# Dilated attention: values as weights in two column halves, output by features

## The chip, the cores and the metric

The kernel runs on one core of one Trainium2 chip, as one launch. The metric is the device time of one execution in microseconds (us); lower is better.

## The reference, cut to what matters

The kernel computes a fixed stack of layers for 256 tokens of width 1024: swiglu blocks, dilated attention, latent attention, windowed grid attention, a gated linear attention and two MLPs. The change lies in the dilated attention:

```
q, k, v = split(x @ w_in, 3)               # 3 groups x 16 heads x 64
q = rope(rmsnorm(q) * q_gain); k = rope(rmsnorm(k) * k_gain)
for g, (window, dilation) in ((128, 1), (512, 4), (2048, 16)):
    o_g, lse_g = softmax attention over t - j * dilation, j = 0 .. window / dilation
wts = softmax(stack(lse_g))                # over the three groups
y = (sum_g wts_g * o_g) @ w_out            # 256 x 1024
```

The weighted sum over the three groups equals one softmax over the scores of all three, with one maximum and one denominator per query and head. The kernel computes it so: 384 scores a row for the first 128 queries (three groups, one key block), 768 for the second 128 (two key blocks).

## The kernel before

Every engine has its own instruction stream, written out by hand in Python; the streams meet only at semaphores (`wait_ge` on a signal and key). Within an engine the order is strict. Nothing is planned at run time.

**Products.** Weights arrive from HBM in chunks of 1 MB. ScalarE rounds a chunk to a high part (`act_begin`, line 439), VectorE forms the low part (`dve_begin`, line 452), and TensorE runs three products for each tile (`mm3`). All products stand in the trace under line 466 (`mm`), all transposes under line 475 (`tr`). An fp32 product leaves two records in the trace, an fp32r product or a transpose one.

**Dilated attention** (lines 1153 to 1418). Four head groups hs of four heads. The loop runs hs from -1 to 3 and i from 0 to 9: at step i TensorE first runs the projection i of head group hs+1 (48 products of 256 columns; i // 3 is the dilation group, i % 3 is q, k or v), then the work of head group hs. So a period of ten steps holds nine projections for the next head group and the whole attention of this one; with hs = 3 there is none, and chunks of an unrelated modulation layer fill the steps 0, 2, 4, 6 (`FILL_DILATED`).

- q and k: ScalarE squares the projection (1285), VectorE sums over a head (1350), GpSimd makes the reciprocal root (1437 to 1446), VectorE scales out of PSUM (1372) and multiplies by the cosine (1374), GpSimd by the sine (1453, 1454), VectorE adds (1377). This is `rotate(hs+1, i)`; in VectorE's stream it is the last thing of step i. TensorE transposes the result (`turn`, at the steps of `DIL_TURN`, line 1139), ScalarE copies it to SBUF (1293).
- `dil_step` numbers eight attention steps s of a head group: pairs s0, s0+1 are two heads of one query block; s // 2 % 2 is the query block tb. At i = 0, 2, 4, 6 TensorE computes `scores` for the pair (the heads in the two row halves of the array), VectorE adds the mask and takes the maximum (1361, 1363), ScalarE exponentiates in place into `aSM` and leaves the row sums in `den` (1302).
- At i = 1, 3, 5, 7 TensorE transposes the exponentials (`turn_p`, three or six 128 x 128 tiles, in groups of three), for both steps of the pair. The groups and the q and k turns alternate between the PSUM banks 5 and 6 (`spare`). VectorE copies the first group to `aPT` (1385), ScalarE the second one (1311).
- `pv` (line 1224): the transposed probabilities are the weights (128 x 128), the values move (64 columns), three or six products per step; the output of all eight steps stands by tokens in bank 7. Step s0 is taken at the even step after, step s0+1 one step later, between the transposes of the next pair.
- At the end of each head group VectorE takes the reciprocal of the eight denominators (1411) and multiplies the output out of PSUM into `aO` (1415, two instructions).

**After the last head group** `attn_out_pe` (1113) turns `aO` to features: 16 transposes into banks 0 to 3, copied as high parts by ScalarE (1103) and low parts by VectorE (1110), then the output projection (96 fp32r products of four chunks in two halves; its first 48 need the tiles 0 to 3 alone).

`x_free`, `h_free` and `grid_sp` hold waits that keep later loads and writes off these buffers.

Of the kernel before, what the change touches and what calls it, by code (L numbers as in the profile page):

```python
# [149 lines left out]
class Program:  # L150
# [106 lines left out]
    def phase_views(self):  # L257
# [12 lines left out]
        self.aO = v(X0, 0, [128, 2048]).rearrange("p (b d) -> p b d", b=2)  # L270
        self.aT = [v(X1, 512 * i, [128, 512]) for i in range(4)]
# [681 lines left out]
    def x_free(self, tag):  # L953

        return {"dil": [(self.turned, ("residual", 0, 3)), (self.v_step, "tables")],
                "f1": [(self.turned, ("dilo", "o", 3))],
# [155 lines left out]

    def attn_out_pe(self, tag, O, ready, w_out):
        self.turn_o_pe(tag + "o", O, ready, 1)
        for half in range(2):
            self.pe_linear(w_out[:, half * 512:half * 512 + 512], self.x_of(tag + "o", 1), 4 * half, 256, (tag, "out", half))
            self.empties(range(4 * half, 4 * half + 4), (self.res, (tag, half)))

    def attn_out_act(self, tag, nxt, at):
        self.turn_o_act(tag + "o", 1)  # L1120
# [4 lines left out]
    def attn_out_dve(self, tag, nxt, at):  # L1125
        self.turn_o_dve(tag + "o", 1)
# [12 lines left out]
    DIL_TURN = {2: (0, 0), 4: (1, 0), 5: (0, 1), 7: (1, 1), 8: (0, 2), 9: (1, 2)}  # L1139
# [13 lines left out]
    def dilated_pe(self):  # L1153
# [57 lines left out]
        def turn_p(hs, s):  # L1211
            nonlocal spare
            u, n = s % 2, 3 * (s // 2 % 2 + 1)
            for c0 in range(0, n, 3):
                b = spare = 11 - spare
                pe.wait_ge(self.expd, ("dil", hs, s))
# [7 lines left out]
        def pv(hs, s):  # L1224
            hd, tb, _ = self.dil_step(s)
            u, hb = s % 2, hs % 2
            nk = tb + 1
            for i in range(3 * nk):
                o, kb = divmod(i, nk)
                g = self.dil_order(s)[o]  # L1230
# [3 lines left out]
                pe.wait_ge(self.evac, ("dil", "v", hs, g))  # L1234
                if s == 0:
                    self.pe_bank(7)
                m = self.mm(PS[:, 7, tb * 256 + hd * 64:tb * 256 + hd * 64 + 64], self.aPT[u][:, i * 128:i * 128 + 128],
                            self.aV[hb][:, g, kb * 256 + hd * 64:kb * 256 + hd * 64 + 64], i == 0, i == 3 * nk - 1)
            m.then_inc(*self.weighed.up(("dil", hs, s)))

        for hs in range(-1, 4):
            for i in range(10):
                if hs + 1 < 4 and i < 9:
                    proj(hs + 1, i)
                if hs + 1 < 4 and i in self.DIL_TURN:
# [3 lines left out]
                if hs >= 0 and i in (1, 3, 5, 7):  # L1249
                    turn_p(hs, i - 1)  # L1250
                    if i > 1:
                        pv(hs, i - 2)
# [3 lines left out]
                if hs >= 0 and i == 8:  # L1256
                    pv(hs, 7)
                if hs == 3 and i in FILL_DILATED:
                    self.pe_mods.send((0, 1))
            if hs >= 0:  # L1260
                self.empties([7], (self.o_done, ("dil", hs)))
        self.attn_out_pe("dil", self.aO, (self.o_done, ("dil", 3)), w_out)

    def dilated_act(self):
# [30 lines left out]
        def score(hs, s):  # L1295
# [4 lines left out]
            if hs:  # L1300
# [1744 lines left out]
```

## Time and profile before

| what | value |
|---|---|
| median of 3 runs | 2511.31 us (2510.83 to 2513.05) |
| profiled execution, its time | 2507.09 us |
| profiled execution, its span | 2505.8 us, mean granted TensorE clock 0.952 |
| TensorE products / weight loads busy | 94% / 86% |
| VectorE / ScalarE / GpSimd busy | 48% / 38% / 21% |
| HBM traffic | 341 MB read, 137 GB/s over the span |

A row of a timeline gives start, duration, engine, line, operation, output <- inputs with shapes, and how often; in brackets stands the time the engine idled before it, and what ended the wait. A matmul's duration contains its way through the array, so consecutive products overlap; what one costs is the distance between starts. PE is TensorE, DVE VectorE, ACT ScalarE, POOL GpSimd. "al" are tiles that share memory (`aSM`, `aPT`, `aV`, `aQK`, `aT`, `aO`), PS is PSUM. The granted clock is the share of 2.4 GHz.

### The profile page before, as it was taken

What the parts mean: (1) busy time and instruction counts of PE and PEld (TensorE: products, weight loads), DVE (VectorE), ACT (ScalarE), POOL (GpSimd) and SP (SyncE); (2) the same over time, 40 slices, a digit from 0 to 9 for tenths busy, and PEclk for the clock granted to TensorE, in tenths of its full rate; (3) what the DMA queues carried; (4) which work ended last, traced back from release to release, by engine and by line L of the source; (5) the groups of instructions that cost most, each with busy time, mean ns of one, the idle gap of its engine ahead of it and who ended that gap; (6) DMA issues with size and microseconds to landing.
All of it is one profiled execution on the core that took longest, in us unless ns stands there. A gap on an engine that the chain in (4) does not pass through costs nothing.

```text
span 2505.8 us, 38228 instructions
## 1 busy us (share of the span) xinstructions
PE 2349.1 (94%) x16869; PEld 2146.4 (86%) x16869; DVE 1211.3 (48%) x1560; ACT 958.5 (38%) x1128; POOL 517.3 (21%) x465
## 2 busy tenths in 40 slices
PE   6999999989999998889999899989999999888998
PEld 6998899979999997557999877877888887668998
DVE  5645566646555553445555355362123254544443
ACT  3433444434433442334444244333222224533442
POOL 2112434402211111220221111012211220220220
PEclk9999999989999998789999899979999989898998
DMA  6555433445555555676554310113233232113551
GB/s 241 177 171 174 136 129 124 135 169 185 182 171 185 185 169 182 217 250 227 180 185 156 105 34 18 35 68 102 100 101 101 86 95 92 59 51 93 182 181 67
DMA packets 205247, 344.75 MB, mean 138 GB/s; under 512 B 8845, under 2 KB 69498, under 8 KB 205082
## 3 DMA queue, kind: packets, MB, share of 16 engines
q1 hardware_dynamic: 205082, 342.31, 41.1%
q8 instruction: 133, 2.18, 0.4%
q14 instruction: 32, 0.26, 0.0%
HBM read 341.24 MB, written 1.05 MB: 137 GB/s over the span
## 4 chain that ended last, share of the span: by engine, by line
PE 81%; DVE 9%; POOL 4%; ACT 3%; issue 2%; SPq 0%; DMA 0%; DVEq 0%; POOLq 0%; ACTq 0%
PE PS L466 78%; PE PS L475 3%; DVE WL L452 3%; ACT WH L439 1%; POOL small L1444 1%; DVE XL L623 1%; POOL TMP L1453 1%; DVE XL L992 0%; DVE al L988 0%; POOL small L1442 0%; DVE TMP L1372 0%; POOL TMP L1454 0%; DVE TMP L1377 0%; DVE al L1901 0%; DVE al L1361 0%
## 5 line engine op out<-in xcount | busy, mean ns | idle before, releaser
L452 DVE TENSOR_TENSOR WL<-raw,WH 128x2048 fp32r<-128x2048 f32 (+2 forms) x281 | 651.4, 2330 | 711.1 <-ACT WH L439 711.0
L466 PE MATMUL PS<-XH,WH 128*128 128x256 f32 (+1 forms) x2336 | 700.7, 300 | 22.9 <-DVE WL L452 14.3
L466 PE MATMUL PS<-XL,WH 128*128 128x256 f32 (+1 forms) x2336 | 694.9, 297 | 0.0
L466 PE MATMUL PS<-XH,WL 128*128 128x256 f32 (+1 forms) x2336 | 694.6, 297 | 0.0
L439 ACT ACTIVATE WH<-raw 128x2048 fp32r<-128x2048 f32 (+2 forms) x281 | 518.9, 1858 | 360.5 <-PE PS L466 359.9
L466 PEld LDWEIGHTS PS<-XH,WH 128*128 128x128 f32 x2336 | 454.1, 194 | 36.6 <-DVE WL L452 15.1
L466 PEld LDWEIGHTS PS<-XL,WH 128*128 128x128 f32 x2336 | 454.5, 195 | 10.0
L466 PEld LDWEIGHTS PS<-XH,WL 128*128 128x128 f32 x2336 | 453.8, 194 | 10.2
L466 PE MATMUL PS<-WH,XH 128*128 128x256 f32 (+2 forms) x944 | 288.3, 305 | 17.8 <-DVE XL L623 8.5
L466 PE MATMUL PS<-WL,XH 128*128 128x256 f32 (+2 forms) x944 | 279.5, 296 | 0.0
L466 PE MATMUL PS<-WH,XL 128*128 128x256 f32 (+2 forms) x944 | 279.2, 296 | 0.0
L466 PE MATMUL PS<-HH,WH 128*128 128x256 f32 x960 | 272.0, 283 | 1.6 <-DVE WL L452 1.6
L466 PE MATMUL PS<-HH,WL 128*128 128x256 f32 x960 | 271.7, 283 | 0.0
L466 PE MATMUL PS<-HL,WH 128*128 128x256 f32 x960 | 271.7, 283 | 0.0
L466 PE MATMUL PS<-al,al 128*128 128x64 f32 (+8 forms) x1376 | 225.4, 342 | 14.8 <-DVE al L2903 4.8
L466 PEld LDWEIGHTS PS<-al,al 128*128 128x128 f32 (+4 forms) x1376 | 164.8, 197 | 63.0 <-issue 37.0
L466 PEld LDWEIGHTS PS<-WH,XH 128*128 128x128 f32 x944 | 186.6, 198 | 36.3 <-issue 22.3
L466 PEld LDWEIGHTS PS<-WL,XH 128*128 128x128 f32 x944 | 187.0, 198 | 2.5
L466 PEld LDWEIGHTS PS<-WH,XL 128*128 128x128 f32 x944 | 186.7, 198 | 2.5
L466 PEld LDWEIGHTS PS<-HH,WH 128*128 128x128 f32 x960 | 184.3, 192 | 1.8 <-DVE WL L452 1.8
L466 PEld LDWEIGHTS PS<-HL,WH 128*128 128x128 f32 x960 | 184.3, 192 | 0.0
L466 PEld LDWEIGHTS PS<-HH,WL 128*128 128x128 f32 x960 | 184.3, 192 | 0.0
(225 smaller groups left out, 2608.7 us busy)
## 6 DMA issues: line engine op xcount, KB each, us to landing
raw<-in_ffn_w_in SPq DMA_DIRECT2D x88, 1024.0 KB, 5.0
raw<-in_w_mod SPq DMA_DIRECT2D x48, 1024.0 KB, 5.1
raw<-in_ffn_w_out SPq DMA_DIRECT2D x40, 1024.0 KB, 4.9
raw<-in_a_w_in SPq DMA_DIRECT2D x36, 1024.0 KB, 4.9
raw<-in_w_mlp_in SPq DMA_DIRECT2D x32, 1024.0 KB, 5.4
raw<-in_w_mlp_out SPq DMA_DIRECT2D x32, 1024.0 KB, 5.0
raw<-in_gla_w_in SPq DMA_DIRECT2D x12, 1024.0 KB, 5.1
raw<-in_attn_w_qkv SPq DMA_DIRECT2D x6, 1024.0 KB, 5.2
```

The source lines that it names most:

```text
L439: act.e.activation(self.WH[q % NW][:, 0:nk * nn], self.raw[j % NRAW][:, 0:nk * nn], ACT.Copy).then_inc(*self.hi.up(j))
L452: dve.e.tensor_tensor(self.WL[j % NRAW][:, 0:nk * nn], self.raw[j % NRAW][:, 0:nk * nn], wh.bitcast(F32), ALU.subtract).then_inc(*self.lo. ...
L466: return self.pe.e.matmul(out, l, r, start=start, stop=stop, skip_group_check=skip)
L475: return self.pe.e.transpose(out, i, self.ident if n == 128 else self.CST[0:n, IDENT:IDENT + n])
L623: dve.e.scalar_tensor_tensor(self.XL[slot][:, k, :], R[:, k, :], self.COL[:, at + k:at + k + 1], self.XH[slot][:, k, :].bitcast(F32), ALU. ...
L1444: pool.e.tensor_tensor(rs, rs, self.MH[:, 0:8], ALU.pow).then_inc(*self.p_step.up(key("pow")))
L1453: pool.e.tensor_tensor(q[:, :, :, 0:32], x[:, :, :, 32:64], bc(0, 32), ALU.mult)
```

## The change

- `pv` takes a pair of steps at once, one step of i later than the first of them could be. The values are now the weights (128 x 64), the probabilities move (128 columns). The even head writes the partitions 0 to 63 of bank 7 and the odd one 64 to 127, so the two lie in the column halves of the array, their products taken in turn. The output stands by features: the same number of products as before.
- As the denominators are per token, the probabilities are divided before they are transposed: `scale` on VectorE takes a reciprocal of two columns and multiplies `aSM` of both steps in place; it stands ahead of everything else at i = 1, 3, 5, 7. `turn_p` on TensorE waits for it instead of the exponential. The reciprocal and the two products at the end of each head group leave VectorE.
- The q turn of the first dilation group moves from i = 2 to i = 3, and `turn_p` of the first step of a pair now stands before the q or k turn of that i.
- ScalarE copies the output of head groups 0 to 2 into `aOT`; high and low parts of these six tiles are made at i = 1, 3, 5 of the last head group, those of the last two straight from bank 7. The 16 transposes before the output projection are gone, for the latent attention they stay.

The core of the diff:

```diff
@@ -1110,20 +1111,35 @@
+    def split_o_act(self, tag, g, h, O, ready):
+        for signal, key in ready:
+            self.act.wait_ge(signal, key)
+        self.act.e.activation(self.XH[h][:, 2 * g:2 * g + 2, :], O, ACT.Copy).then_inc(*self.xh.up((tag, 2 * g)))
+    def split_o_dve(self, tag, g, h, O):
+        self.dve.wait_ge(self.xh, (tag, 2 * g))
+        self.dve.e.tensor_tensor(self.XL[h][:, 2 * g:2 * g + 2, :], O, self.XH[h][:, 2 * g:2 * g + 2, :].bitcast(F32), ALU.subtract).then_inc(*self.xl.up((tag, 2 * g)))
+        self.xl.name((tag, 2 * g + 1))
     def attn_out_pe(self, tag, O, ready, w_out):
-        self.turn_o_pe(tag + "o", O, ready, 1)
+        if O is not None:
+            self.turn_o_pe(tag + "o", O, ready, 1)
         for half in range(2):
...
     def attn_out_act(self, tag, nxt, at):
-        self.turn_o_act(tag + "o", 1)
+        if tag == "lat":
+            self.turn_o_act(tag + "o", 1)
         for half in range(2):
...
     def attn_out_dve(self, tag, nxt, at):
-        self.turn_o_dve(tag + "o", 1)
+        if tag == "lat":
+            self.turn_o_dve(tag + "o", 1)
         for half in range(2):
@@ -1136,7 +1152,7 @@
-    DIL_TURN = {2: (0, 0), 4: (1, 0), 5: (0, 1), 7: (1, 1), 8: (0, 2), 9: (1, 2)}
+    DIL_TURN = {3: (0, 0), 4: (1, 0), 5: (0, 1), 7: (1, 1), 8: (0, 2), 9: (1, 2)}
...
@@ -1213,7 +1229,7 @@
                 b = spare = 11 - spare
-                pe.wait_ge(self.expd, ("dil", hs, s))
+                pe.wait_ge(self.v_step, ("dil", "scaled", hs, s))
                 self.pe_bank(b)
...
                     m = self.tr(PS[:, b, i * 128:i * 128 + 128], self.aSM[u][:, (c0 + i) * 128:(c0 + i) * 128 + 128])
@@ -1221,45 +1237,47 @@
-        def pv(hs, s):
-            hd, tb, _ = self.dil_step(s)
-            u, hb = s % 2, hs % 2
+        def pv(hs, s0):
+            hb, tb = hs % 2, s0 // 2 % 2
             nk = tb + 1
-            for i in range(3 * nk):
-                o, kb = divmod(i, nk)
-                g = self.dil_order(s)[o]
+            if s0 == 0:
+                self.pe_bank(7)
+            for s in (s0, s0 + 1):
                 pe.wait_ge(self.emptied, ("dil", "p", hs, s))
...
                     pe.wait_ge(self.evac, ("dil", "p", hs, s))
-                pe.wait_ge(self.evac, ("dil", "v", hs, g))
-                if s == 0:
-                    self.pe_bank(7)
-                m = self.mm(PS[:, 7, tb * 256 + hd * 64:tb * 256 + hd * 64 + 64], self.aPT[u][:, i * 128:i * 128 + 128],
-                            self.aV[hb][:, g, kb * 256 + hd * 64:kb * 256 + hd * 64 + 64], i == 0, i == 3 * nk - 1)
-            m.then_inc(*self.weighed.up(("dil", hs, s)))
+            for i in range(3 * nk):
+                o, kb = divmod(i, nk)
+                for s in (s0, s0 + 1):
+                    hd, _, _ = self.dil_step(s)
+                    pair, j = divmod(hd, 2)
+                    g = self.dil_order(s)[o]
+                    pe.wait_ge(self.evac, ("dil", "v", hs, g))
+                    m = self.mm(PS[64 * j:64 * j + 64, 7, pair * 256 + tb * 128:pair * 256 + tb * 128 + 128], self.aV[hb][:, g, kb * 256 + hd * 64:kb * 256 + hd * 64 + 64],
+                                self.aPT[s % 2][:, i * 128:i * 128 + 128], i == 0, i == 3 * nk - 1, True)
+                    if i == 3 * nk - 1:
+                        m.then_inc(*self.weighed.up(("dil", hs, s)))
...
                     proj(hs + 1, i)
+                if hs >= 0 and i in (1, 3, 5, 7):
+                    turn_p(hs, i - 1)
                 if hs + 1 < 4 and i in self.DIL_TURN:
...
                 if hs >= 0 and i in (1, 3, 5, 7):
-                    turn_p(hs, i - 1)
-                    if i > 1:
-                        pv(hs, i - 2)
                     turn_p(hs, i)
...
                     pv(hs, i - 2)
-                if hs >= 0 and i == 8:
-                    pv(hs, 7)
                 if hs == 3 and i in FILL_DILATED:
...
             if hs >= 0:
-                self.empties([7], (self.o_done, ("dil", hs)))
-        self.attn_out_pe("dil", self.aO, (self.o_done, ("dil", 3)), w_out)
+                self.empties([7], (self.xl, ("dilo", 6)) if hs == 3 else (self.evac, ("dil", "o", hs)))
+        self.attn_out_pe("dil", None, None, w_out)
@@ -1297,8 +1315,6 @@
             act.wait_ge(self.v_step, ("dil", "neg", hs, s))
-            if hs:
-                act.wait_ge(self.v_step, ("dil", "recip", hs - 1))
             act.e.activation(SM, SM, ACT.Exp, bias=nm[:, u:u + 1], accum_out=den[:, tb * 4 + hd:tb * 4 + hd + 1]).then_inc(*self.expd.up(("dil", hs, s)))
...
         def turn_p(hs, s):
@@ -1309,6 +1325,9 @@
             act.e.activation(self.aPT[s % 2][:, 384:768], PS[:, b, 0:384], ACT.Copy).then_inc(*self.evac.up(("dil", "p", hs, s)))
+        def split(g):
+            self.split_o_act("dilo", g, 1, self.aOT[:, 2 * g:2 * g + 2, :], [(self.evac, ("dil", "o", g)), (self.lin, ("dil", 3, 8))])
...
             for i in range(10):
@@ -1328,6 +1347,15 @@
                     self.fill_act(0)
+                if hs == 3 and i in (1, 3, 5):
+                    split(i // 2)
+            if hs >= 0:
+                o = PS[:, 7, :].rearrange("p (k t) -> p k t", k=2)
+                if hs == 3:
+                    self.split_o_act("dilo", 3, 1, o, [(self.weighed, ("dil", 3, 7)), (self.lin, ("dil", 3, 8))])
+                else:
+                    act.wait_ge(self.weighed, ("dil", hs, 7))
+                    act.e.activation(self.aOT[:, 2 * hs:2 * hs + 2, :], o, ACT.Copy).then_inc(*self.evac.up(("dil", "o", hs)))
         self.attn_out_act("dil", "f1", 16)
@@ -1384,11 +1412,22 @@
+        def scale(hs, s0):
+            hd, tb, _ = self.dil_step(s0)
+            dve.wait_ge(self.expd, ("dil", hs, s0 + 1))
+            dve.e.reciprocal(rd[:, 0:2], den[:, tb * 4 + hd:tb * 4 + hd + 2]).then_inc(*self.v_step.up(("dil", "recip", hs, s0)))
+            dve.wait_ge(self.v_step, ("dil", "recip", hs, s0))
+            for s in (s0, s0 + 1):
+                SM = self.aSM[s % 2][:, 0:384 * (tb + 1)]
+                dve.e.tensor_scalar(SM, SM, rd[:, s - s0:s - s0 + 1], None, ALU.mult).then_inc(*self.v_step.up(("dil", "scaled", hs, s)))
         self.past_norm = None
...
                 if paired:
+                    scale(hs, i - 1)
                     turn_p(hs, i - 1)
...
                     self.dve_begin()
@@ -1405,16 +1444,9 @@
                     self.dve_mods.send(1)
-            if hs < 0:
-                continue
-            dve.wait_ge(self.weighed, ("dil", hs, 7))
-            dve.e.reciprocal(rd, den).then_inc(*self.v_step.up(("dil", "recip", hs)))
-            dst = self.aO[:, :, hs * 256:hs * 256 + 256].rearrange("p b (h d) -> p b h d", h=4)
-            dve.wait_ge(self.v_step, ("dil", "recip", hs))
-            for tb in range(2):
-                t = dve.e.tensor_tensor(dst[:, tb], PS[:, 7, tb * 256:tb * 256 + 256].rearrange("p (h d) -> p h d", h=4),
-                                        rd[:, 4 * tb:4 * tb + 4].unsqueeze(2).to_broadcast([128, 4, 64]), ALU.mult)
-            t.then_inc(*self.o_done.up(("dil", hs)))
+                if hs == 3 and i in (1, 3, 5):
+                    self.split_o_dve("dilo", i // 2, 1, self.aOT[:, i - 1:i + 1, :])
+        self.split_o_dve("dilo", 3, 1, PS[:, 7, :].rearrange("p (k t) -> p k t", k=2))
         self.attn_out_dve("dil", "f1", 16)
```

## Rows read from the trace of the kernel before

**Rows 1.** The page, part 1: busy time, share of the span, instructions.

```profile
PE 2349.1 (94%) x16869; PEld 2146.4 (86%) x16869; DVE 1211.3 (48%) x1560; ACT 958.5 (38%) x1128; POOL 517.3 (21%) x465
```

**Rows 2.** Busy time by stretch: length, busy (instructions), PEclk, DMA share, GB/s.

```profile
373.00:447.00 74.00, 72.14 (x618) 69.97 (x616) 48.07 (x68) 34.13 (x48) 29.93 (x36) 1.00 0.39 129
...
545.90:552.50 6.60, 6.53 (x30) 6.36 (x30) 0.57 (x2) 0.98 (x2) 0.00 (x0) 0.50 0.00 0
...
557.00:563.00 6.00, 6.00 (x52) 6.00 (x52) 3.68 (x3) 2.43 (x3) 0.00 (x0) 1.00 0.00 0
```

**Rows 3.** Waits of TensorE, 366 to 440 us: total, times, longest.

```profile
PE PS L475 <- ACT al L1311: 1.5, 1, 1.5
```

**Rows 4.** Timeline of TensorE, one period.

```profile
372.55 0.94 PE L466 MATMUL PS<-al,al 64*128 64x128 f32 x12
373.42 0.39 PE L466 MATMUL PS<-WH,XH 128*128 128x256 f32 x1
...
379.26 0.82 PE L475 MATMUL PS<-CST,al 128*128 128x128 f32 x6
...
437.59 2.79 PE L466 MATMUL PS<-al,al 128*128 128x64 f32 x24
440.22 0.61 PE L475 MATMUL PS<-CST,TMP 128*128 128x128 f32 x4
```

**Rows 5.** Timeline of VectorE, the same period.

```profile
379.39 0.69 DVE L1377 TENSOR_TENSOR TMP<-TMP,al 128x512 f32<-128x512 f32 x1 [1.39 <-POOL TMP L1454]
...
414.18 0.69 DVE L1377 TENSOR_TENSOR TMP<-TMP,al 128x512 f32<-128x512 f32 x1 [1.37 <-POOL TMP L1454]
...
427.28 0.69 DVE L1377 TENSOR_TENSOR TMP<-TMP,al 128x512 f32<-128x512 f32 x1 [1.40 <-POOL TMP L1454]
...
430.21 0.69 DVE L1350 TENSOR_REDUCE small<-al 128x8 f32<-128x512 f32 x1 [0.23 <-ACT al L1285]
...
436.93 0.69 DVE L1377 TENSOR_TENSOR TMP<-TMP,al 128x512 f32<-128x512 f32 x1 [1.39 <-POOL TMP L1454]
```

**Rows 6.** Timeline of VectorE and TensorE, last head group, step i = 7.

```profile
545.23 0.55 DVE L1385 COPY al<-PS 128x384 f32<-128x384 f32 x1
545.92 1.51 PE L475 MATMUL PS<-CST,al 128*128 128x128 f32 x6 [5.11 <-DVE al L1385]
```

**Rows 7.** The chain that ended last: start, us, what; one period, then the end.

```profile
398.03 5.75 PE PS L466 x48
...
430.28 0.62 PE PS L466 x6
...
437.76 2.63 PE PS L466 x24
...
547.44 5.03 PE PS L466 x24
552.49 0.21 DVE small L1411
...
552.73 0.77 DVE al L1415 x2
...
553.54 3.59 PE PS L475 x16
557.12 42.96 PE PS L466 x359
```

**Rows 8.** Timeline of TensorE: a fill by modulation.

```profile
521.55 1.06 PE L466 MATMUL PS<-raw,CS 128*32 128x512 f32 x8
```

**Rows 9.** Instructions by line and shape, whole span: busy, mean ns.

```profile
L1686 DVE TENSOR_SCALAR al<-al,small 128x384 f32<-128x384 f32 x2 | 0.8, 416 | 16.2 <-POOL small L1796 16.2
...
L1686 DVE TENSOR_SCALAR al<-al,small 128x256 f32<-128x256 f32 x2 | 0.7, 346 | 0.0
```

**Rows 10.** Timeline of ScalarE, the period of group 4.

```profile
394.58 0.18 ACT L1302 ACTIVATION_READ_ACCUMULATOR al<-al,small 128x1 f32 x1
...
440.86 0.60 ACT L1293 ACTIVATE al<-PS 128x512 f32<-128x512 f32 x1 [1.74 <-PE PS L475]
```

More of the change, by code:

```diff
@@ L270, in phase_views @@
         self.aO = v(X0, 0, [128, 2048]).rearrange("p (b d) -> p b d", b=2)
+        self.aOT = self.tiles(v(X0, 0, [128, 2048]))
         self.aT = [v(X1, 512 * i, [128, 512]) for i in range(4)]
@@ L955, in x_free @@
         return {"dil": [(self.turned, ("residual", 0, 3)), (self.v_step, "tables")],
-                "f1": [(self.turned, ("dilo", "o", 3))],
+                "f1": [(self.xl, ("dilo", 5))],
                 "f2": [(self.lin, ("f1", "up", 5))],
@@ L2240, in grid_sp @@
     def grid_sp(self):
-        self.sp.wait_ge(self.o_done, ("dil", 3))
+        self.sp.wait_ge(self.xl, ("dilo", 6))
         self.sp.e.dma_start(self.CST[:, 0:1024], self.A["const"][:, MASK_C:MASK_C + 1024]).then_inc(*self.ld_masks.up("grid"))
```

## The prediction

> **What bounds the kernel now.** I read the page, then the busy time by stretch, the waits of TensorE, and the timelines of one 74 us period of the dilated attention. TensorE's matmuls are busy 94% of the span [rows 1]. A period (attention of head group hs beside the nine projections of hs+1) repeats every 74 us with TensorE busy 72.14 of them, at the full clock (granted 1.00, 2.4 GHz) [rows 2]; there are three. In a period TensorE waits 1.5 us at one place [rows 3], and nowhere else as long as half of that. So in these periods the instructions in TensorE's queue set the time, and whatever delays one of them longer than those waits adds to it. VectorE is busy 48 us, but its order is fixed, and it waits for GpSimd inside every rotation: it finishes rotate(0) at 380.08 where TensorE finished the projection of i=1 at 379.26 [rows 4, 5]. Today that costs nothing, since the transposes of the probabilities need only the exponential. The last head group has no projections beside it: there TensorE waits 5.11 us for VectorE's copy of step 6, its clock is 0.50 (1.2 GHz) behind that, and after the last value product stand 4.6 us before the output projection [rows 2, 6, 7].
>
> **The value products.** 72 records a period (two per product; 3 products per step with one key block, 6 with two). The eight steps cost 4 x 0.62 + 4 x 1.3 = 7.7 us: six records take 0.62, twelve half of the 24 in 2.63 [rows 7], which the timeline shows as 2.79 with the end of the last one [rows 4]. After: 128 moving columns instead of 64, weights of 64 columns, two heads side by side in the array's halves. Such a form is not in the trace. Nearest rows: the scores, which pair two heads in the row halves with the same 128 moving columns: 12 records from 372.55 to the next product at 373.42, 0.87 us [rows 4]; and modulation's four column quarters, eight records of 512 columns in 1.06 us, near a quarter of the 3.4 they would need one by one, two passes each at 2.4 GHz, 0.43 a record [rows 8]. I take 0.9 us for a pair of one-block steps and, for twice the records with one entry and exit of some 0.3 us, 1.5 us for a pair of two-block steps: 2 x 0.9 + 2 x 1.5 = 4.8 us, a gain of 2.9 us a period. Bounds: nothing overlaps, 72 records of 0.107 us or 7.7 (gain 0); perfect overlap, half of it, 3.85 (gain 3.85).
>
> The Trainium skill speaks against it a little: "TensorEngine Tiling (Array Packing)", section Tiling Modes, says that a change of the tiling mode drains the array. Every pair would pay that on entry and exit. The scores' 0.87 us already holds two changes of mode, so the sum stays; had it to be paid on top, the gain would be nearer to the lower bound.
>
> **The scaling on VectorE.** Added per pair: a reciprocal (0.21, the wait behind it makes 0.24 [rows 7]) and two in-place multiplications of 384 or 768 elements. The nearest row is the multiplication of line 1686, SBUF to SBUF by a column: 0.416 us for 384 elements, 0.346 for 256 [rows 9]; 128 elements more cost 0.07, so 768 cost 0.416 + 3 x 0.07 = 0.63. Starts follow each other some 0.08 earlier. So step s0 is ready 0.7 us (0.95 with two blocks) after the scaling begins, VectorE is free after 0.95 (1.35). Bounds: free (0) and the PSUM copy's pace, 0.55 for 384 [rows 6] and near 0.95 for 768. Removed: one reciprocal and two multiplications out of PSUM at the end of each head group, 1.0 us of VectorE [rows 7]; added on ScalarE one 0.6 us copy of the outputs per head group, behind a product long done and beside the next projection: nothing, with several us idle there as cover.
>
> **Where TensorE now waits, for one period** (before, after, by shifting the rows):
> - i=1. The scaling stands behind rotate(0): starts 380.00, step 0 ready 380.72; TensorE asked at 379.26. Wait 1.5. All behind it moves 1.3 to 1.5, rotate(1) too.
> - i=2. The q turn (0.45) leaves, the pair costs 0.9 instead of 0.62: -0.15. Projection 3 now ends 395.4.
> - i=3. The exponential of step 3, 394.76 before [rows 10], comes at 396.06, since VectorE reaches the masks 1.3 later. Scaled step 2: 397.0, wait 1.6. Six transposes until 397.7. The q turn now stands here: its bank needs VectorE's copy (from 397.6, since three transposes end 0.5 us after their start, six taking 0.82 with starts 0.11 apart [rows 4], to 398.1), it runs to 398.57. ScalarE, in order, copies the turn (its copy starts 0.64 behind the turn, 440.22 to 440.86, and takes 0.5 before the next can start [rows 4, 10]), squares projection 3 (0.5) and only then empties (0.5) the bank that step 3 needs: 400.3. Step 3 is done at 400.95; before, the projection behind it stands in the chain from 398.03 [rows 7], and its first product began 0.25 earlier, beside the end of the transposes: 397.78: +3.2 in all, +2.0 by this step.
> - i=4 and 5. Rotate(3) ends near 407.1 (its square comes late, 399.9, then 7.3 as the shortest such rotation shows, 430.21 to 437.62 [rows 5]). It pushes rotate(4) from 414.87 to 416.05; scaled step 4 is ready 416.7, TensorE asks at 415.4. Wait 1.3, and 0.35 more for the one bank, in place of step 3's product (1.3): +0.4.
> - i=6: +0.15. i=7: rotate(6) ends 431.5, scaled step 6 almost in time (0.15), but turn, square and evacuation queue on ScalarE as at i=3 (1.7), less step 5's product: +1.05.
> - i=8: one pair of 1.5 for the 24 records in 2.63: -1.1.
>
> Sum 1.5 - 0.15 + 2.0 + 0.4 + 0.15 + 1.05 - 1.1 = +3.85 us a period, three periods +11.5. The 2.9 us of TensorE work saved are already in it.
>
> **The last head group and its end.** Up to step 6 the scaling's waits (about 1 us a pair) are paid by the shorter products and the fills of modulation as cover: 0. At i=7 VectorE is free at 545.23 as before; steps 6 and 7 are scaled at 546.1 and 546.6; transposes, two copies and evacuations at the half clock bring step 7's probabilities to 549.6. The product pair, 24 records, takes 3.0 us where it took 5.03 at that clock: until 552.7, as before 552.47. Then the output projection starts at once, where it stood until 557.12 behind 0.24 + 0.8 + 3.59 us [rows 7]: the transposes of the outputs are gone, and the split of the last two tiles lies beside the first 5.76 us of the projection, as long as one of 48 products [rows 7]. But the clock stays low until about 557 (it did after the wait of 5.11; the new wait is 6.9), so 4.4 us earlier are worth half: 2.1. The first six tiles' splits move into i=1, 3, 5 (0.6 on ScalarE, 0.7 on VectorE): they lie beside the fills. The mask load on SyncE waits for a later signal, far ahead of its use: nothing.
>
> Sum: +11.5 - 2.1 = +9.4 us. The profiled execution took 2507.1 us (span 2505.8), 4.2 below the median 2511.3; on that the forecast is 2520.7.
>
> **Rivals.**
> - *TensorE's work decides (faster).* Place: i=1, 3, 5, 7 of each period. If the scaling is hidden, the four groups keep 4 x 2.9 and the end gives 2 to 4.6: -14 to -16 us, about 2496. It decides where the waits added per period stay under the 2.9 saved. For it: VectorE idles 26 us a period [rows 2]. Against: it idles inside rotations, ahead of the scaling, not behind; the 1.5 us at i=1 needs no estimate beyond 0.7. 0.14.
> - *Even.* The bank queue at i=3 and 7 costs only half (ScalarE takes the evacuation first, or the shift of rotate(3) is absorbed): 3 x 1.5 - 2.1 = +2.4 us: 2513.7. 0.16.
> - *The clock falls in each period.* In 395.4 to 400.3 TensorE would stand 3.8 us. Rows show 0.50 for 6.6 us behind the wait of 5.11 us and 1.00 again from 557 on, while the period with the 1.5 us wait stays at 1.00 [rows 2, 3, 6]. If it falls once a period for as long as those 6.6 us, half of that is lost: 3 x 3.3 = +10 more, 2531. The Trainium skill, "TensorE: Matmul & The Clock Gate", section What's actually happening, calls the low clock the default that activity lifts; by that rule alone the low level would come back with these pauses; the rows show it behind the long one only. 0.12.
> - *The change's new form brings no overlap in the column halves.* Products cost 7.7 again: i=6 and 8 lose 1.35 more a period, the end 2: +6, 2527. It lies inside the forecast's sign. 0.08.
>
> **How the numbers follow.** Forecast as such 0.50; rivals as given. The forecast's own range is 2514 to 2528 (1 to 1.8 us a period either way from the scaling's and pair's bounds). With the others, 2504 to 2532 leaves out the faster rival's core and little above. Slower by over 0.2% (5 us, about what a measurement can tell): 0.50 of the forecast less 0.04 for its lower edge, the clock's 0.12, the missing overlap's 0.08 and a quarter of the even case, 0.04: 0.70. Within: the rest of these two, 0.16. Faster: 0.14.
>
> **What would show it.** Right: periods near 78 us; per period new waits of TensorE before transposes for VectorE's multiplication (1.5 at i=1) and for ScalarE's evacuation (1.7 at i=3 and 7); product pairs at 0.9 and 1.5; multiplications 0.42 and 0.63; no transposes between last product and projection, with the clock low across it. Wrong: periods under 74 us, or waits at i=3 without ScalarE in them.

## The result, and the profile after

The kernel with the change takes 2533.34 us (median of 4: 2527.25, 2529.35, 2537.32, 2537.54), the kernel before beside it 2511.07 (2510.68 to 2513.05): ratio 1.0079 with a 95% interval of [1.0055, 1.0103] (the two medians by themselves give 1.0089), 22 us slower. The forecast said slower, 2520.7 us; the median lies 1.3 us above its range. Run again later, five times beside nine runs of before, the same kernel took 2523.15 (2518.75 to 2525.74) against 2508.64: 1.0052 [1.0039, 1.0065], 14.5 us slower. Two of the four first runs, the profiled one among them (2537.54 and 2537.32), thus held some 12 us more than the slowest of those five.

The profiled run took 2537.54 us, 30.4 more than before's 2507.09. By stretches, from the same instruction to the same instruction in both traces:

| stretch | before | after | difference |
|---|---|---|---|
| up to the first exponential of the dilated attention | 300.7 | 303.2 | +2.5 |
| period 1, exponential to exponential | 73.97 | 79.96 | +6.0 |
| period 2 | 73.95 | 79.22 | +5.3 |
| period 3 | 68.67 | 75.11 | +6.4 |
| from there to the last weight load of the stage | 45.6 | 41.6 | -4.0 |
| grid attention, load to load, which the change doesn't touch | 141.4 | 155.3 | +13.9 |
| all the rest | | | +0.3 |

(Period 3 is short in both, as the first exponential of the last head group has no projection ahead of it.) So the dilated attention itself costs +13.7 us: +17.7 in three periods, -4.0 in the last head group. The +2.5 ahead of it lies before the attention of the first head group and need not be the change's: the traces of all kernels here start that exponential between 300.7 and 303.3 us, the kernel before reordered (e12) at 303.1.

Page of after, part 1 (answers to [rows 1]):

```profile
PE 2359.9 (93%) x16853; PEld 2144.0 (85%) x16853; DVE 1226.2 (48%) x1596; ACT 960.0 (38%) x1131; POOL 514.3 (20%) x465
```

The page hardly shows it: the shares are those of before. It takes the stretches. Busy time by stretch of after (columns as in [rows 2]): the three periods, then stretches of low clock in them (the four falls, the one of period 3 at i = 3 first), the end of the last head group, then one stretch of the grid attention:

```profile
303.24:383.20 79.96, 72.58 (x614) 68.04 (x613) 51.70 (x78) 34.52 (x48) 28.78 (x37) 0.96 0.36 119
383.20:462.42 79.22, 71.84 (x614) 67.47 (x613) 51.76 (x78) 34.59 (x48) 28.79 (x37) 0.98 0.36 120
462.42:537.53 75.11, 66.94 (x564) 61.91 (x566) 44.43 (x74) 28.57 (x44) 27.75 (x34) 0.95 0.37 123
...
487.50:490.90 3.40, 2.63 (x13) 2.66 (x14) 2.40 (x3) 1.71 (x4) 2.11 (x4) 0.51 0.03 9
409.00:412.40 3.40, 3.35 (x16) 3.38 (x17) 2.68 (x3) 1.81 (x2) 2.83 (x4) 0.51 0.00 0
327.10:333.90 6.80, 5.15 (x26) 4.78 (x24) 4.26 (x5) 3.77 (x5) 3.29 (x5) 0.50 0.22 72
525.10:528.50 3.40, 3.40 (x18) 3.40 (x17) 1.68 (x3) 0.49 (x1) 2.43 (x4) 0.50 0.04 14
...
562.60:572.80 10.20, 5.53 (x36) 4.72 (x36) 5.45 (x8) 1.78 (x4) 0.00 (x0) 0.50 0.26 90
...
1569.60:1600.30 30.70, 30.35 (x122) 21.86 (x120) 13.45 (x61) 10.01 (x30) 0.00 (x0) 0.50 0.00 1
```

Two things differ from before. TensorE is idle 7.4 us of a period instead of 1.9. And the granted clock of a period is no longer 1.00: it is 0.50 for 6.8, 3.4 and 6.8 us of the three. In the grid attention one stretch of 30.7 us runs at 0.50 with TensorE busy throughout; before is at 1.00 in that stage.

Where TensorE idles in period 2, its waits (answers to [rows 3]):

```profile
PE PS L476 <- ACT al L1327: 3.3, 2, 1.7
PE PS L476 <- DVE al L1423: 2.9, 3, 1.4
PE PS L476 <- DVE al L1413: 1.1, 3, 0.4
```

7.3 us, of the three kinds that the forecast named: the multiplication (line 1423), VectorE's copy that empties the one free bank (1413), ScalarE's evacuation behind turn and square (1327). One by one, timeline of TensorE in period 3:

```profile
468.42 0.88 PE L476 MATMUL PS<-CST,al 128*128 128x128 f32 x6 [1.25 <-DVE al L1423]
...
484.70 0.88 PE L476 MATMUL PS<-CST,al 128*128 128x128 f32 x6 [1.42 <-DVE al L1423]
485.99 0.63 PE L476 MATMUL PS<-CST,TMP 128*128 128x128 f32 x4 [0.41 <-DVE al L1413]
488.27 1.51 PE L476 MATMUL PS<-CST,al 128*128 128x128 f32 x6 [1.65 <-ACT al L1327]
...
505.07 0.55 PE L476 MATMUL PS<-CST,al 128*128 128x128 f32 x3 [0.27 <-DVE al L1423]
...
506.37 0.52 PE L476 MATMUL PS<-CST,al 128*128 128x128 f32 x3 [0.31 <-DVE al L1413]
...
522.17 0.63 PE L476 MATMUL PS<-CST,TMP 128*128 128x128 f32 x4 [0.41 <-DVE al L1413]
524.45 0.92 PE L476 MATMUL PS<-CST,al 128*128 128x128 f32 x6 [1.65 <-ACT al L1327]
...
532.91 1.53 PE L467 MATMUL PS<-al,al 128*64 128x128 f32 x24
```

i = 1, 3, 5, 7 in turn. And ScalarE at i = 3, why the bank is late: turn copy, square, evacuation, one after the other.

```profile
486.66 0.60 ACT L1311 ACTIVATE al<-PS 128x512 f32<-128x512 f32 x1 [1.06 <-PE PS L476]
487.15 0.59 ACT L1303 ACTIVATE al<-PS 128x512 f32<-128x512 f32 x1
487.63 0.50 ACT L1327 ACTIVATE al<-PS 128x384 f32<-128x384 f32 x1
```

What was added and made cheaper, by line and shape, period 2:

```profile
L467 PE MATMUL PS<-al,al 128*64 128x128 f32 x72 | 4.8, 278 | 0.0
...
L1423 DVE TENSOR_SCALAR al<-al,small 128x768 f32<-128x768 f32 x4 | 2.3, 618 | 0.1
...
L1423 DVE TENSOR_SCALAR al<-al,small 128x384 f32<-128x384 f32 x4 | 1.5, 418 | 0.1
```

The end of the last head group, timeline of TensorE (answers to [rows 6, 7]):

```profile
566.50 3.15 PE L476 MATMUL PS<-CST,al 128*128 128x128 f32 x12 [6.71 <-DVE al L1423]
570.32 2.76 PE L467 MATMUL PS<-al,al 128*64 128x128 f32 x24 [0.67 <-ACT al L1327]
573.01 0.39 PE L467 MATMUL PS<-XH,WH 128*128 128x256 f32 x1
```

The projection starts right behind the last value products, as meant, and the clock is back at 1.00 when it starts. (In the later profile of the same kernel, e14, it comes back 1.9 us into the projection.)

### The profile page after: what moved, and what is told of

Read it like the earlier page. It is cut to its first block, busy times and chain, and to the rows that moved or that the text cites. A ratio compares the mean times of both kernels' runs of the same rounds, so it can differ in the third digit from the quotient of the medians.

```text
span 2536.2 us, 38232 instructions
## 1 busy us (share of the span) xinstructions
PE 2359.9 (93%) x16853; PEld 2144.0 (85%) x16853; DVE 1226.2 (48%) x1596; ACT 960.0 (38%) x1131; POOL 514.3 (20%) x465
## 3 DMA queue, kind: packets, MB, share of 16 engines
HBM read 341.24 MB, written 1.05 MB: 135 GB/s over the span
## 4 chain that ended last, share of the span: by engine, by line
PE 80%; DVE 9%; POOL 5%; ACT 4%; issue 2%; SPq 0%; DMA 0%; DVEq 0%; POOLq 0%; ACTq 0%
PE PS L467 76%; PE PS L476 4%; DVE WL L453 3%; POOL small L1476 1%; ACT WH L440 1%; POOL TMP L1485 1%; DVE XL L624 1%; DVE TMP L1400 0%; POOL TMP L1486 0%; DVE TMP L1405 0%; DVE XL L993 0%; DVE small L1378 0%; POOL small L1474 0%; DVE al L1389 0%; DVE al L989 0%
## 5 line engine op out<-in xcount | busy, mean ns | idle before, releaser
L467 PE MATMUL PS<-al,al 128*128 128x64 f32 (+9 forms) x1376 | 220.1, 358 | 13.7 <-DVE al L2930 7.4
L467 PEld LDWEIGHTS PS<-al,al 128*128 128x128 f32 (+4 forms) x1376 | 154.4, 195 | 67.0 <-issue 41.4
```

Source lines behind the costliest of these rows:

```text
L467: return self.pe.e.matmul(out, l, r, start=start, stop=stop, skip_group_check=skip)
```

## The experiments

**Theories.** A: the fixed order of the queues. The multiplication stands behind a whole rotation, and the turn ahead of the second group of transposes; these make the waits, and moving the two makes them go. B: the work itself costs (VectorE's added time, or a product form without overlap), wherever it stands. C: the clock falls because of the new stands, or by itself.

To compare the runs I split the middle one of the three periods (first exponential of a head group to that of the next) into TensorE's waits, half of the time at clock 0.50 (what that level costs a busy TensorE), and the rest, which is TensorE's own work. The split is good to about 1 us, since some of the low time falls into waits. Within that, the rest is the same wherever the work is the same (68.6 to 70.3 with the paired products in turn, 72.0 to 72.6 with the products of before), so nothing else sets the period. The last two columns are for the whole stage: the time at 0.50 in all three periods, and the time from the first exponential to the output projection. Times of whole kernels that ran once carry up to 6 us of other stages, so the stage is the safer comparison:

| kernel | us | middle period | waits | at 0.50 | rest | at 0.50, three periods | stage |
|---|---|---|---|---|---|---|---|
| before | 2508.6 | 73.95 | 1.9 | 0 | 72.1 | 0 | 256.2 |
| after | 2523.2 | 79.22 | 7.3 | 3.4 | 70.2 | 17.0 | 269.8 |
| e1 | 2519.8 | 79.30 | 7.3 | 6.8 | 68.6 | 27.2 | 268.6 |
| e2 | 2514.4 | 78.70 | 6.7 | 3.4 | 70.3 | 6.8 | 264.7 |
| e3 | 2514.2 | 75.97 | 4.7 | 3.4 | 69.6 | 10.2 | 258.2 |
| e4, not divided | 2504.2 | 74.52 | 5.1 | 0 | 69.4 | 10.2 | 254.8 |
| e8, not divided | 2506.2 | 74.43 | 4.8 | 0 | 69.6 | 3.4 | 250.3 |
| e5 | 2534.1 | 81.87 | 6.8 | 6.8 | 71.7 | 20.4 | 278.1 |
| e7 | 2529.0 | 79.69 | 5.4 | 3.4 | 72.6 | 17.0 | 277.8 |
| e10, e13 | 2491.7 | 70.71 | 1.7 | 0 | 69.0 | 0 | 237.2, 238.1 |
| e11, not divided | 2485.6 | 70.14 | 1.2 | 0 | 68.9 | 0 | 232.3 |
| e12 | 2506.8 | 73.35 | 1.4 | 0 | 72.0 | 0 | 250.3 |

(us: of before, after and e13 the medians of the last series; the others ran once, e10 also once, at 2487.72. Before, beside the single runs, took 2506.1 to 2506.4 in the first two series. After's split is of the first profile; its later one, e14, has a middle period of 79.12, the same waits, 13.6 us at 0.50 in the three periods and a stage of 268.9.)

**e1: the multiplication earlier.** On VectorE, from ahead of the transposes to ahead of the rotation of the step before.

```diff
+                    scale(hs, i)
                 if hs + 1 < 4 and i < 9 and i % 3 < 2:
                     rotate(hs + 1, i)
...
-                    scale(hs, i - 1)
```

> The changed kernel, with the scaling moved in VectorE's stream from the head of the odd step to behind the masks of the even step, ahead of rotate. Theory A (fixed orders of VectorE and ScalarE make the waits, the multiplications themselves are cheap): TensorE's wait of 1.25 us at i=1 and the 0.3 at i=5 vanish, the 1.4 at i=3 stays since it hangs on the exponential, the two of 1.65 for ScalarE's evacuation stay; the middle period, 79.2 us now with 1.7 of them from a fall of the clock, comes to 75.5 to 77. Theory B (the scaling costs its time wherever it stands, since VectorE has no room in a period): the wait moves to the rotations and the period stays within 1 us of 79.2.

2519.82 us. Waits of the middle period:

```profile
PE PS L476 <- ACT al L1327: 3.3, 2, 1.6
PE PS L476 <- DVE al L1413: 2.0, 3, 1.3
PE PS L476 <- DVE al L1423: 2.0, 1, 2.0
```

The wait at i = 1 is gone, yet the sum is again 7.3: the copy of line 1413 now waits behind the rotation instead (1.3), and at i = 3 the exponential and its multiplication come late by 2.0, behind VectorE's split of the weights (line 453, 2.2 us). One move exposes what stood next in the same queue. The middle period, 79.30, is what theory B expected.

**e2: the second group of transposes ahead of the turn**, on TensorE; on ScalarE the turn's copy then stands behind both evacuations (not shown).

```diff
                     turn_p(hs, i - 1)
+                    turn_p(hs, i)
                 if hs + 1 < 4 and i in self.DIL_TURN:
                     turn(hs + 1, i)
-                    turn_p(hs, i)
```

> The changed kernel, with the q and k turns of the odd steps behind both probability transposes on TensorE, and on ScalarE both evacuations ahead of the turn's copy. Theory A: the two waits of 1.65 us for ScalarE and the waits of 0.4 for VectorE's copy shrink to some 0.5 each pair, the middle period comes to 74 to 75.5, and the falls of the clock at i=3 vanish as no stand of over 2 us is left. Theory B: the wait for the multiplications (2.9 a period) grows by what the others lose, period 77 or more.

2514.39 us: no wait for ScalarE's evacuation is left (3.3 before), but waits for the multiplication grow to 4.7, as the transposes at i = 5 now stand 2.0 us. Again the middle period, 78.70, is in the range of theory B (77 or more), and the clock still falls in two of the three periods, now behind that stand.

**e3: both.** 

> Both moves in one kernel. Theory A: the middle period falls below the 73.95 of the kernel before, to 72 to 73.5, with no fall of the clock in the three periods; the wait that stays is the one for scaled step 2 at i=3, some 1 us. Theory B: it stays above 75. The last head group is as in the changed kernel in either.

2514.17 us, middle period 75.97. The waits fall by more than by either alone, to 4.7:

```profile
PE PS L476 <- DVE al L1415: 2.7, 4, 1.3
PE PS L476 <- DVE al L1425: 2.0, 1, 2.0
```

But not under the 73.95 of before, which I had expected of theory A; 75.97 is once more in the range of B (above 75). The late split ahead of step 3 and the copies behind rotations remain. So these three runs alone don't decide between A and B: the waits lie where A puts them, but they move on instead of going. What decides are the runs without the division and the full reordering, e10 and e11. The stage is 2.0 us longer than before's; the other 6 us by which e3 is slower lie outside it.

**e4 and e8: the division left out** (the output is then not divided by the denominators), in after's order and in e2's.

```diff
-                pe.wait_ge(self.v_step, ("dil", "scaled", hs, s))
+                pe.wait_ge(self.expd, ("dil", hs, s))
...
-                    scale(hs, i - 1)
```

> The changed kernel without the division: no reciprocal and no multiplication, the transposes wait for the exponential again, so the output is left undivided. The order of turns, the paired products and the new end stay. Theory A: the 2.9 us of waits for the multiplications go, the two waits of 1.65 for ScalarE stay, middle period 74 to 75.5. Theory B: nearly all waits come from the scaling, middle period 71 to 72.5 (73.95 less the 2.9 the products save). The clock then does not fall in either.

> No division (output left undivided) and the turns behind both transposes: what the paired products are worth with little in their way. Theory A: waits for ScalarE vanish, those for VectorE's copies behind rotate at i=5 and 7 stay (1 to 2 us a period); middle period 71.5 to 73, below the 73.95 of before, no fall of the clock. If it stays at 74 or more, the products' saving of 2.9 us is not there.

2504.17 and 2506.16 us. Without the division e4's periods are 2.5, 4.7 and 4.5 us shorter than after's, low clock included (of the middle one's 4.7, 2.2 are waits and 1.7 clock), and still 5.1 us of waits for bank and copies stand in the middle one. That is the range of theory A (74 to 75.5). I had expected no fall of the clock; it fell in the first period for 6.8 us and in the third for 3.4. e8 missed its expectation (71.5 to 73, no fall): the copies behind rotations wait 3.0 in five places, ScalarE's evacuation 1.8 in one, and the third period has 3.4 us at 0.50. By its own words a period of 74 or more would deny the products' saving; the rest of 69.6 for before's 72.1 shows it all the same, with e10 and e12 below.

**e5: the column halves not in turn.** All products of one head, then those of the other; same count and form.

```diff
-            for i in range(3 * nk):
-                o, kb = divmod(i, nk)
-                for s in (s0, s0 + 1):
+            for s in (s0, s0 + 1):
+                for i in range(3 * nk):
+                    o, kb = divmod(i, nk)
```

> The changed kernel, with the products of a pair not taken in turn: all of the even head, then all of the odd one. Theory 1 (the two column halves overlap, which needs the turns): 24 records take 2.6 us instead of 1.46 and 12 take 1.35 instead of 0.9; about 1.4 us of the 3.2 show in the middle period (80.6), since those at i=2 and 4 lie ahead of a wait for the multiplication. Theory 2 (the products are cheaper because their weight loads have 64 columns, not because two run at once): 24 records stay near 1.5.

2534.14 us. By line and shape, and one pair in the timeline:

```profile
L467 PE MATMUL PS<-al,al 128*64 128x128 f32 x72 | 7.2, 278 | 0.0
...
454.86 2.46 PE L467 MATMUL PS<-al,al 128*64 128x128 f32 x24
```

7.2 us instead of 4.8, 2.46 instead of 1.53 for a pair of 24 records, and a middle period 2.65 us longer (81.87, where 80.6 was expected). The overlap is there, and it comes from the turns.

**e7: the kernel before with the division in after's place**, and nothing else of the change.

> The kernel before with one part of the change alone: the probabilities are divided by VectorE ahead of each pair's copies, the transposes wait for that, and the end of a head group copies the output instead of multiplying it. Products, turns, transposes of the output as before. Theory A (what costs is where the scaling stands in VectorE's order): new waits for the multiplication of 1.3 at i=1, 1.5 at i=3 and 2 at i=5 where the transposes now stand behind rotate; middle period 77.5 to 79, the end unchanged or 1 later. Rival (the changed kernel's loss came from the moved turns): period 75 or less.

2529.04 us, 22.6 more than before beside it, so at least as slow as after. Waits of its middle period, the longest one in the timeline, and the stretch at low clock behind it:

```profile
PE PS L475 <- DVE al L1392: 5.0, 3, 2.7
PE PS L475 <- ACT al L1293: 0.4, 1, 0.4
...
424.39 0.55 PE L475 MATMUL PS<-CST,al 128*128 128x128 f32 x3 [2.65 <-DVE al L1392]
...
425.20:428.60 3.40, 3.40 (x19) 3.40 (x18) 1.24 (x3) 0.00 (x0) 0.00 (x0) 0.50 0.15 49
```

The multiplication at that place alone makes a loss of this size, and with it the clock falls (17.0 us at 0.50 in three periods). Here each fall comes at i = 5 behind one stand of 2.65 us, with no other in the 17 us ahead of it. The middle period, 79.69, is a little over the expected 77.5 to 79.

**e10: all that the waits pointed to.** The multiplication ahead of the rotation (at i = 2 also ahead of the weight split); the second transposes ahead of the turns; the turns at steps without transposes; both groups of probabilities copied by ScalarE; in the last head group the weight splits of one fill a step later on ScalarE and VectorE.

```diff
-    DIL_TURN = {3: (0, 0), 4: (1, 0), 5: (0, 1), 7: (1, 1), 8: (0, 2), 9: (1, 2)}
+    DIL_TURN = {2: [(0, 0)], 4: [(1, 0)], 6: [(0, 1), (1, 1)], 8: [(0, 2)], 9: [(1, 2)]}
...
-            act.wait_ge(self.turned, ("dil", "p", hs, s, 3))
+            for c0 in (0, 3) if s // 2 % 2 else (0,):
+                act.wait_ge(self.turned, ("dil", "p", hs, s, c0))
...
-                if hs == 3 and i in FILL_DILATED:
+                if hs == 3 and i in (0, 2, 4, 7):
...
+                    scale(hs, i)
+                    if i == 2 and hs + 1 < 4:
+                        self.dve_begin()
```

> The change with its queues reordered, same results: scaling behind the masks and ahead of rotate, at i=2 also ahead of the weight split; all copies of probabilities on ScalarE, off VectorE; q and k turns at even steps only (2, 4, 6, 6, 8, 9); in the last head group the weight splits of the fill at i=6 come one step later on ScalarE and VectorE. Theory A: waits per period under 2 us, middle period 71 to 73 (before 73.95), the 6.7 us stand of the last head group falls under 2 and with it the fall of the clock there; stage end 15 to 20 us earlier than in the changed kernel, the whole near 2495 against 2506 before. Rival (ScalarE, now with 0.5 us for every group of transposes, becomes what is waited for): period 74 to 76.

2487.72 us. The middle period and its waits:

```profile
373.45:444.16 70.71, 68.98 (x614) 65.90 (x613) 47.14 (x70) 37.49 (x56) 30.93 (x37) 1.00 0.41 135
```

```profile
PE PS L476 <- ACT al L1322: 1.0, 2, 0.5
PE PS L476 <- DVE TMP L1402: 0.7, 1, 0.7
```

TensorE's work sets the period again, 3.2 us shorter than before, at clock 1.00 throughout, and the period is just under the expected 71 to 73. In the last head group the 6.7 us stand is gone; the longest is now 2.6 us, for a weight split ahead of the output projection.

**e13 and e14: e10 and the change, timed together.**

> The reordered change once more, with the division, timed in five rounds. Its one look gave 2487.7 us beside 2506.4 for the kernel before, with the middle period at 70.7 us instead of 73.95. If that is the mechanism and not one lucky run, the ratio is 0.991 to 0.994 with an interval clear of 1.

> The changed kernel again, unaltered, for its spread: its four executions were 2527, 2529, 2537 and 2538 us, and the profiled one (2537.5) had the clock at its low level for 30.7 us in the grid attention, a stage that the change doesn't touch. If that fall comes by chance of timing, the executions fall into two groups 8 to 12 us apart, told by the mean granted clock (0.939 against 0.945 to 0.947), and the upper group is absent or present at random; if the change causes it, all executions lie at 2537.

e13: 2491.74 us (2487.57 to 2494.29) against 2508.64, ratio 0.993 [0.9916, 0.9943]: faster than both kernels, with an interval clear of 1. e14: 2523.15, as told above. In e14's profile the grid attention runs at the full clock but for 3.4 us near its end:

```profile
1470.90:1613.40 142.50, 132.82 (x970) 108.58 (x969) 78.49 (x289) 66.93 (x167) 13.84 (x24) 0.99 0.07 23
```

142.5 us from load to load, where before took 141.4 and the first profile of after 155.3. So of nine executions of after at most two had the long stretch. None of before's 16 on record lies above 2513.05, so whether the change makes such a stretch likelier stays open.

**e11 and e12: what of e10 is worth what.** e11 leaves the division out of e10 (output not divided, as in e4). e12 is the kernel before with e10's turns, ScalarE's copies and its fill, without pairs and division.

> The reordered change without reciprocals and multiplications (output left undivided): what the division still costs once its place is right. Theory A: nothing that TensorE sees, middle period within 0.5 us of 70.7. Rival (the division always costs a latency): 1 to 2 us less, 69 to 69.7, which is TensorE's own work.

> The kernel before with the same reordering but without the change: probabilities copied by ScalarE, turns at the even steps, the fill's weight splits of i=6 one step later; products by tokens, division at the end, transposes of the output. If the gain of the reordered change comes from its paired products and its end, this one keeps a period of 72 to 73.5 (73.95 less the waits of 1.9) and the stage ends 8 to 14 us behind the reordered change. If the gain is only the order, it reaches 70.7 as well.

e11: 2485.63 us, periods 69.91, 70.14, 64.62 against e10's 70.69, 70.71, 64.61: well placed, the division costs at most 0.8 us a period. In the last head group, which has no projections beside it, it still costs 3.6 us (from its first exponential to the output projection 31.2 with the division and 27.7 without; TensorE waits for it three times, 3.5 us in all). e12: 2506.79 us, periods 73.36, 73.35, 68.09: the order alone gives 0.6 a period. Its middle period waits once:

```profile
PE PS L475 <- ACT al L1307: 1.4, 1, 1.4
```

From e12 to e10 lie 2.7, 2.6 and 3.5 us, with about the same waits in both (1.4 and 1.7 in the middle period): that is what the paired products bring once little waits. The last head group brings 4.3 more (35.5 and 31.2).

## Why the prediction was right and wrong

**The bound of before: right.** Whatever delays an instruction in TensorE's queue lengthens the period. The table bears it out: own work, waits and low clock make up every period.

**The waits: right, place by place.** Period 3 shows at i = 1 1.25 us (forecast 1.5), at i = 3 1.42, 0.41 and 1.65 (1.6, a bank wait of 0.4, 1.7), at i = 7 0.41 and 1.65 (0.15 for the multiplication did not come; 1.7). At i = 5 0.27 and 0.31 stand for 1.3 and 0.35: here the forecast was too high. It had pushed rotate(4) by 1.2 us through a late square. In period 2 of after that rotation does end late, 42.4 us behind the first exponential where before has 40.2, but TensorE is late too: it asks at 42.7, where the forecast had 40.7. The low clock ahead of it, 3.4 us, is part of that, so the clock hid some of this wait. Less half of the time at the low clock, the periods grew by 2.6, 3.6 and 3.0 us, where the sum said 3.85 each: 9.2 in all for 11.5. Waits and work taken apart give much the same: the stands that the forecast lists come to 8.7 us a period, 6.8 more than before's 1.9, and were to be lessened by 2.9 of products; the middle period shows 5.4 more of waits and 1.9 less of work. (The term of +1.05 at i = 7 does not follow from its own words: 0.15 and 1.7 less step 5's product, which with one key block is 0.6, make 1.25.)

**The value products: right.** 4.8 us (forecast 4.8), a pair of two-block steps 1.46 in the chain (1.5). The form brings overlap, and e5 ends the rival that it does not. The Trainium skill's rule that a change of tiling mode drains the array ("TensorEngine Tiling (Array Packing)", section Tiling Modes) left the sum as it was. This trace shows no price for it apart: the 1.53 us of a pair hold its entry and exit, and the pairs cost what the sum had given them.

**The multiplications: right** (0.618 and 0.418 us for 0.63 and 0.42).

**The clock: the step that failed.** The sum took each period at granted clock 1.00, so its term for the clock was nothing, and it gave the case that the clock falls once a period 0.12. It fell in each: 17.0 us at 0.50 in three periods (13.6 in e14's profile). Half of that is 8.5 us (7.3, if only the 14.5 us count in which TensorE was busy); the rival had 10. The waits and the clock both came, 9.2 and 8.5 of the 17.7 us by which the periods grew, so the rival was not an alternative to the forecast but a term that belonged into it. The forecast reasoned from the single wait of 1.5 us that before bears without a fall [rows 2, 3]. But at i = 3 three stands of 1.42, 0.41 and 1.65 follow one another, with 0.9 and 0.6 us of transposes between them, and the clock goes to 0.50 inside the last of them (487.5; in period 1 the low level begins at about 327, just ahead of the last). In all three periods the fall begins 24 to 26 us after the first exponential, that is at i = 3; in period 3 another comes at i = 7, again behind stands of 0.41 and 1.65 (not so in e14's profile). The forecast had listed these stands, 3.8 us in five; it should have given the fall the larger chance. That stands bring the falls, and not the chip by itself (theory C), fits all kernels here: in the 15 periods of before, e10, e11, e12 and e13, none of whose stands is longer than 1.5 us, the clock never falls, and every fall in the others comes with a stand of 1.3 us or more in it or right ahead. But the stands do not fix it: e4 has the same one of 2.28 us in all three periods and falls there in two of them. The Trainium skill has such a case, in "TensorE: Matmul & The Clock Gate", section A second HAM failure mode: psum-queue depth-cycling: frequent short idles between groups of matmuls, as PSUM banks are cycled, make the clock go up and down. This case agrees in part: two of the three stands wait for a bank, the first one for the multiplication. The forecast weighed another section of that page, and by long pauses alone.

**The end: right, term too small.** -4.0 us for -2.1. The stand was 6.71 us (6.9). The term halved its gain for a clock that would stay low until long into the projection, as after before's pause; it was back at 1.00 at 572.8, 6.3 us after TensorE resumed, before the projection began, while before bore 0.50 for 13.7 us. So the sign that the forecast named, a low clock across the projection's start, did not show in this profile. In e14's it did, 8.5 us after TensorE resumed, and the gain was 4.0 there too; what the halving should have been replaced by stays open.

**What no step held.** 13.9 us of the first profile are the grid attention's 30.7 us at clock 0.50, with TensorE busy in 30.35 of them. e14 is the same kernel and its profile shows nothing of it, so it is not a fixed part of the change's price. That the other of the two long runs, 2537.32, had it too is likely from its time and its mean granted clock (0.939 for both, 0.945 and 0.947 for the two shorter ones), but only one of the two has a trace. Without it: 2527 to 2529 us in the first series and 2523 in the second, a growth of 14.5 to some 17.

**Against the rivals.** "TensorE's work decides" was wrong for this order and right for e10, whose 2491.74 (-16.9) is near what it would have given (-14 to -16). "Even" would have needed a bank queue of half the size; it had 1.65 for 1.7 both times.

The sum of the forecast by its measured terms: +9.2 waits and products, +8.5 clock and -4.0 end make +13.7 in the stage, and the second series measured +14.5 in all. That the forecast of +9.4 lies as near to this as it does is in part luck: 2.3 us too much of waits and 1.9 us too little at the end made up for half of the clock that it left out.

What stays open: why e1's fall lasted longer than after's (6.8 for 3.4 us in the middle period) with the same sum of waits, and what the low stretch in the grid attention comes from.

## What to carry to other kernels

Where one engine's fixed queue sets the time, a new instruction on another engine costs what stands ahead of it there, not what it takes: the same division cost 2.5 to 4.7 us a period behind a rotation, low clock included, and at most 0.8 ahead of it, with the other queues set in order too. Where nothing else filled TensorE, in the last head group, it kept its 3.6 us even so. Move it together with everything that waits in the same row, as single moves hand the wait to the next in line (e1), and judge the change only then: here that turned +14.5 us into -16.9. And give the clock a term of its own where TensorE gets new stands: several short ones with little between them, or one of 2 to 3 us, brought it to half here, though not each time, and that cost nearly as much as the waits themselves.

## What was not expected of the hardware

- Stands of 1.42, 0.41 and 1.65 us with transposes in between brought the granted clock to 0.50 in each period, and so did a single one of 2.65 us (e7). A single 1.5 us did not, nor did the 1.7 us of e10's middle period, in three places. A stand of 2.28 us (e4) did in two periods of three.
- Products with 64 weight columns in the two column halves cost 4.8 us for 72 records when the halves alternate and 7.2 when they don't; with all 128 columns and 64 moving it was 9.1 (e12, same work). These are busy times, which for the last form hold more than the distances between starts, 7.7 by the forecast's rows.
- A stretch of 30.7 us at clock 0.50 came with TensorE busy 99% of it, in a stage whose mean granted clock was 0.99 in the same kernel's other profile.
